# Four more matrices and whole down projections in split fp32r products, expert biases added by TensorE

## The reference, cut to what matters

```
# end of block 1 and of the mixer of block 2
x = x + concat([hm, ha]) @ w_out                  # 1024 x 1024
mix = (gate_a * y_a + gate_b * y_b) @ w_out_2     # 1024 x 1024
# block 3
proj = x @ w_in_3                                 # 1024 x 2048: pool value, b gate, c gate, conv value
mix = concat([y_pool, y_conv]) @ w_out_3          # 1024 x 1024
x = layer_norm(ALPHA * x + mix)
# mixture of experts: 32 experts, top 4, rows sorted into blocks of 128 of one expert each
gu = xb @ w_gu[e] + b_gu[e]                       # 128 x 1024 @ 1024 x 2048
gate = min(gu[:, :1024], 7);  up = clip(gu[:, 1024:], -7, 7)
yb = ((up + 1) * gate * sigmoid(1.702 * gate)) @ w_dn[e] + b_dn[e]
```

## Time and profile before

| | |
|---|---|
| median of 3 runs | 3586.9 us |
| profiled execution, its time and its span | 3590.4 us, 3588.6 us |
| TensorE busy in the span | 3244.0 us (90%) |
| VectorE, ScalarE, GpSimd busy | 53%, 41%, 16% |
| mean granted TensorE clock | 0.951 |
| the expert stage, about 2195 to 3420 us | VectorE near 85% busy, DMA near 400 GB/s |

### The profile page before, as it was taken

How to read it: one execution, slowest core, us unless ns; L and a number is a source line. 1 busy time by engine, 2 the same in 40 slices (tenths; PEclk the granted TensorE clock), 3 DMA queues, 4 the chain that set the end, 5 groups by cost and what they waited for, 6 DMA issues and landing times. The chain is left out here.

```text
span 3588.6 us, 37970 instructions
## 1 busy us (share of the span) xinstructions
PE 3244.0 (90%) x13384; PEld 2295.1 (64%) x13384; DVE 1889.2 (53%) x2272; ACT 1484.3 (41%) x1959; POOL 563.6 (16%) x305
## 2 busy tenths in 40 slices
PE   7977899998999796979998985999999999999976
PEld 6744488784455675658886445777777777777752
DVE  3266233513344405160033236888888888888825
ACT  4344244422445321132232013656656656656522
POOL 3400144440000342124442000000000000000010
PEclk9988999999999797999999987999999999999988
DMA  3333222231111121212235307999999999999840
GB/s 137 111 148 141 94 73 104 81 112 64 59 70 47 55 96 61 94 47 94 94 117 214 117 33 312 392 402 404 393 404 398 400 406 397 400 405 397 360 199 24
DMA packets 69954, 713.66 MB, mean 199 GB/s; under 512 B 7408, under 2 KB 7792, under 8 KB 29424
## 3 DMA queue, kind: packets, MB, share of 16 engines
q1 hardware_dynamic: 58704, 670.10, 47.1%
q0 software_dynamic: 7056, 25.69, 1.8%
q10 hardware_dynamic: 4112, 16.78, 1.2%
HBM read 672.17 MB, written 40.37 MB: 199 GB/s over the span
## 5 line engine op out<-in xcount | busy, mean ns | idle before, releaser
L136 POOL TENSOR_TENSOR ring_low<-ring,ff_ring_high 128x1024 fp32r<-128x1024 f32 x136 | 331.0, 2466 | 734.5 <-ACT ff_ring_high L131 734.5
L197 PE MATMUL psum<-ff_high,ff_ring_high 128*128 128x512 f32 x832 | 326.2, 392 | 23.1 <-DVE h_low L337 8.6
L199 PE MATMUL psum<-ff_high,ring_low 128*128 128x512 f32 x832 | 325.4, 391 | 0.0
L197 PE MATMUL psum<-ex_high,ex_rows_high 128*128 128x512 f32 x768 | 316.3, 412 | 6.8 <-DVE ring_low L2518 6.8
L199 PE MATMUL psum<-ex_high,ex_rows_low 128*128 128x512 f32 x768 | 301.9, 393 | 0.0
L198 PE MATMUL psum<-h_low,ff_ring_high 128*128 128x512 f32 x704 | 275.3, 391 | 0.0
L2518 DVE TENSOR_TENSOR ex_more_low<-ex_more,ex_high_in_x 128x2048 fp32r<-128x2048 f32 x96 | 219.4, 2286 | 70.4 <-ACT ex_high_in_x L2445 70.4
L2518 DVE TENSOR_TENSOR ring_low<-ring,ex_high 128x2048 fp32r<-128x2048 f32 x96 | 214.2, 2287 | 40.3 <-ACT ex_high L2445 40.3
L1497 PE MATMUL psum<-h,ring 128*128 128x512 f32 x512 | 224.0, 594 | 1.1 <-ACTq L1568 1.1
L2407 PE MATMUL psum<-ex_more,ex_act_t 128*128 128x512 f32 x512 | 224.9, 592 | 0.0
L2445 ACT ACTIVATE ex_high<-ex_more 128x1024 fp32r<-128x1024 f32 x192 | 200.8, 1063 | 57.3 <-PE psum L199 57.3
(11 more groups left out here) (512 smaller groups left out, 6440.0 us busy)
## 6 DMA issues: line engine op xcount, KB each, us to landing
ex_more<-moe_w SPq DMA_DIRECT2D x128, 2048.0 KB, 10.5
ring<-wstream SPq DMA_DIRECT2D x87, 2048.0 KB, 8.1
ring<-moe_w SPq DMA_DIRECT2D x64, 2048.0 KB, 11.8
ex_bias_up<-moe_b SPq DMA_DIRECT2D x32, 1024.0 KB, 8.3
y_rows<-ex_y SPq DMA_DIRECT2D x33, 512.0 KB, 9.0
y_rows<-mx_zero ACTq DMA_DIRECT2D x1, 16384.0 KB, 51.5
ex_bias_down<-moe_b SPq DMA_DIRECT2D x32, 512.0 KB, 8.3
x<-xt SPq DMA_DIRECT2D x8, 256.0 KB, 5.9
```

Of the source, the lines that this page charges most:

```text
L136: e.tensor_tensor(low, full, high.bitcast(F32), ALU.subtract).then_inc(self.low_ready, 1)
L197: pe.matmul(out, a[0], b[0], start=start, stop=False)
L199: return pe.matmul(out, a[1], b[0], start=False, stop=stop)
```

## The change

- `w_out`, `w_out_2`, `w_in_3` and `w_out_3` join `SPLIT` and are computed as split products. `Halves` makes the halves of an activation that no norm precedes, at the head of `out1` and `out2`. The mixer's norm gets halves (`keep` also keeps x itself), VectorE makes the low half of the first panel in between and GpSimd those of the later panels; the mixed tiles are split at the end of each panel's step, the low half on GpSimd.
- Expert stage: all 24 quarters are split, through a ring of twelve high quarters. The order is 0 to 15 as before, then (4,0), (4,1), (5,0), (5,1), (4,2), (4,3), (5,2), (5,3). The fp32 products are gone.
- VectorE now makes the low pairs n = 20 and 22 after `low_act(0)` and `take_up(1)`, and only then comes to `low_rows(0)`, `low_act(1)`, `low_rows(1)`.
- The biases are split once in `route_stage`, stored as two rows for each expert, and loaded as two rows; TensorE adds them with one fp32r matmul of ones for each bank (six a block). The steps that take the banks lose their bias operand, and `take_gate` and `take_up` one instruction each.

```diff
-SPLIT = ("w_in", "w_up", "w_down", "w_mix_a", "w_zv", "w_mix_b", "w_ffn_in", "w_ffn_out")
+SPLIT = ("w_out_3", "w_in_3", "w_out_2", "w_out", "w_in", "w_up", ... "w_ffn_out")
+class Halves:
+    def finish(self, act, t):
+        act.activation(tile_of(self.high, t), tile_of(self.full, t), ACT.Copy).then_inc(self.high_ready, 1)
+    def apply(self, dve, between):
+        for t in range(DT):
+            if between is not None:
+                between(t)
+            dve.wait_ge(self.high_ready, t + 1)
+            dve.tensor_tensor(tile_of(self.low, t), tile_of(self.full, t), tile_of(self.high, t).bitcast(F32), ALU.subtract)\
+                .then_inc(self.low_ready, 1)
 def dense_stage(...)  # ScalarE
+                if norm is not None and norm.interleave:
+                    for c in range(PARTS):
+                        if dve_lows:
+                            ring.high_part(act, n0, c)
+                        norm.finish(act, 2 * c)
+                        norm.finish(act, 2 * c + 1)
 def mixer_stage(...)  # GpSimd
+                norm.wait_tile(pool, DT - 1)
+                ring.low_done = n0 + 1
+                ring.low_until(pool, n0 + 3)
+                for j in range(4):
+                    low_tile(j, 2 * j + 1)
+                    low_tile(4 + j, 2 * j + 2)
+                    ring.low_until(pool, min(n0 + j + 4, n0 + 5))
 def route_stage(...)  # SyncE, behind the six pieces of the first expert
+                sp.wait_ge(bias_high_ready, 1)
+                sp.dma_start(r.bias_halves[:, 0, :], bias_high[:, :].bitcast(F32)).then_inc(bias_stored, 16)
+                sp.wait_ge(bias_low_ready, 1)
+                sp.dma_start(r.bias_halves[:, 1, :], bias_low[:, :].bitcast(F32)).then_inc(bias_stored, 16)
+                sp.wait_ge(bias_stored, 32)
 def expert_stage(...)
-    RING = 10
+    RING = 12
-    PIECES = ... + tuple((s, c) for s in (4, 5) for c in range(2))
+    PIECES = ... + tuple((s, 2 * a + c) for a in range(2) for s in (4, 5) for c in range(2))
-    act_at, dve_at = (14, 19), (8, 10, 14, 18)
+    act_at, dve_at = (14, 19, 20), (8, 10, 14, 18, 20)
 # TensorE
+                def add_bias(s, bank, added):
+                    at = (0, 2, 1, 3)[s] if s < 4 else s
+                    mm = pe.matmul(bank, ones[:, :], bias[:, at * PANEL:(at + 1) * PANEL], start=True, stop=False)
...
                     pe.wait_ge(h_done, b * 2 + 4)
                     turn_act(1)
                     pe.wait_ge(x_low, b * 2 + 3)
                     turn_rows(1)
                     for c in range(2):
                         quarter(b, 5, c, psum[:, 7, :], act_high, act_low)
-                    pe.wait_ge(a_ready, b + 1)
+                    pe.wait_ge(a_low, b * 2 + 2)
                     for s in (4, 5):
-                        for k in range(4, KT):
-                            mm = pe.matmul(psum[:, s + 2, :], act_t[:, k - 4, :], weights(s, k), start=False, stop=k == KT - 1)
-                        mm.then_inc(dn_done, 1)
+                        for c in (2, 3):
+                            quarter(b, s, c, psum[:, s + 2, :], act_high, act_low)
 # ScalarE
+                        if n == act_at[2]:
+                            sigmoid(b, 1)
...
-                    sigmoid(b, 1)
                     act.wait_ge(x_turned, b * 2 + 3)
                     high_rows(0)
-                    take_act(b)
+                    high_act(b, 1)
 # VectorE
                 def take_gate(b, c):
-                    dve.tensor_tensor(gate[:, :], psum[:, 2 * c, :], bias_up[:, 512 * c:512 * c + 512], ALU.add).then_inc(taken, 1)
-                    dve.tensor_scalar(gate[:, :], gate[:, :], SW_LIMIT, None, ALU.min).then_inc(limited, 1)
+                    dve.tensor_scalar(gate[:, :], psum[:, 2 * c, :], SW_LIMIT, None, ALU.min).then_inc(taken, 1)
...
+                        if n == dve_at[4]:
+                            low_act(b, 0)
+                            take_up(b, 1)
                         dve.wait_ge(high_ready, b * NQ + n + 2)
                         at = slice(c * PART, (c + 2) * PART)
                         dve.tensor_tensor(low_piece(s)[:, at], piece(s)[:, at], slots(n, 2).bitcast(F32), ALU.subtract)\
                             .then_inc(low_ready, 1)
-                    low_act(b)
-                    take_up(b, 1)
-                    for c in range(2):
-                        low_rows(b * 2 + 2 + c, c)
+                    low_rows(b * 2 + 2, 0)
+                    low_act(b, 1)
+                    low_rows(b * 2 + 3, 1)
```

More of the change, by code:

```diff
@@ L125, in split_parts, with high_part @@
             yield self.tile[:, n % SLOTS, part], self.high[:, n % SLOTS, part], self.low[:, n % SLOTS, part]
+    def high_part(self, act, n, c):
+        act.wait_ge(self.landed[n % SLOTS], 16 * (n // SLOTS + 1))
+        full, high, _ = list(self.split_parts(n))[c]
+        act.activation(high, full, ACT.Copy).then_inc(self.high_ready, 1)
     def high_panel(self, act, n, more=0):
@@ L378, in apply_raw, with __init__, wait_tile, averages @@
             dve.scalar_tensor_tensor(xt, xt, self.before(t), self.var, ALU.mult, ALU.mult).then_inc(self.raw_scaled, 1)
+class Halves:
+    def __init__(self, sem, name, full, high, low):
+        self.full, self.high, self.low, self.before, self.interleave = full, high, low, None, True
+        self.high_ready, self.low_ready = sem(f"{name}_high"), sem(f"{name}_low")
+    def wait_tile(self, e, t):
+        e.wait_ge(self.low_ready, t + 1)
+    def averages(self, pe):
+        pass
+    def finish(self, act, t):
+        act.activation(tile_of(self.high, t), tile_of(self.full, t), ACT.Copy).then_inc(self.high_ready, 1)
+    def deviations(self, dve):
+        pass
+    def apply(self, dve, between):
[5 more added lines that the diff above has]
+                .then_inc(self.low_ready, 1)
 class Tile:
@@ L1428, in block_1 @@
             Tile([n0 + t // 4], t % 4 * P, P, h, None, "dve",
-                 (lambda to: lambda e, bank: e.tensor_tensor(to, bank, to, ALU.add))(x[:, t, :])) for t in range(DT)],
-            n0 + 2 + SLOTS, split_to=FIRST["w_up"] + 1,
+                 (lambda to: lambda e, bank: e.tensor_tensor(to, bank, to, ALU.add))(x[:, t, :]), halves=(high, g.h_low))
+            for t in range(DT)],
+            n0 + 2 + SLOTS, split_to=FIRST["w_up"] + 1, dve_lows=True,
+            norm=lambda sem, scratch: Halves(sem, "mix", h, high, g.h_low),
             sums=lambda sem, buf, final: Sums(g, sem, x, buf, final, False))
@@ L1943, in _ @@
                 norm.averages(pe)
[L1944 removed]
                 for k in range(KT):
+                    ring.wait_part(pe, n0, k)
                     norm.wait_tile(pe, k)
                     for m in range(4):
[L1948 removed]
+                        mm = split_product(pe, psum[:, m, :], ring.halves(n0, k, m * P, P), tile_halves(x_high, x_low, k),
+                                           k == 0, k == KT - 1)
                         if k == KT - 1:
@@ L2072, in route_stage @@
         norm = norm(sem, in_row[:, :, :].rearrange("p (a c) r -> p a (c r)", a=4))
+        bias, bias_low = with_low(nc, own, "rt_bias", [NE, 3 * D])
+        bias_high = nc.alloc_sbuf_tensor_at("rt_bias_high", [NE, 3 * D], F32R, offset=g.h_at)
+        bias_in, bias_high_ready, bias_low_ready, bias_stored = (sem(n) for n in (
+            "bias_in", "bias_high_ready", "bias_low_ready", "bias_stored"))
         logit_taken = sem("logit_taken")
@@ L2750, in block_3 @@
     r.blanked = g.kept.enter_context(nc.semaphore("y_blanked"))
-    mixer_stage(g, x, h, r)
-    n0 = FIRST["w_out_3"]
-    dense_stage(g, "out3", [
-        Tile([n0 + t // 4], t % 4 * P, P, h, None, "dve",
-             (lambda to: lambda e, bank: e.tensor_tensor(to, bank, to, ALU.add))(x[:, t, :])) for t in range(DT)], n0 + 2, scale_x=x,
-                sums=lambda sem, buf, final: Sums(g, sem, x, buf, final, True))
+    r.bias_halves = nc.dram_tensor("bias_halves", [NE, 2, 3 * D], F32, kind="Internal").ap()
+    with ExitStack() as own:
+        high = g.open_split(own, "b3")
+        with nc.sbuf_tensor("b3_x_high", [P, DT, S], F32R) as x_high, nc.sbuf_tensor("b3_x_low", [P, DT, S], F32R) as x_low:
+            mixer_stage(g, x, h, r, high, x_high, x_low)
+        n0 = FIRST["w_out_3"]
+        dense_stage(g, "out3", [
+            Tile([n0 + t // 4], t % 4 * P, P, h, None, "dve",
+                 (lambda to: lambda e, bank: e.tensor_tensor(to, bank, to, ALU.add))(x[:, t, :]), halves=(high, g.h_low))
+            for t in range(DT)], n0 + 2, scale_x=x, split_to=n0 + 2,
+                    sums=lambda sem, buf, final: Sums(g, sem, x, buf, final, True))
     with ExitStack() as own:
```

169 lines of the change are left out of this document (100 added, 69 removed).

## The result

The changed kernel takes 3726.6 us (median of 4 runs, 3724.4 to 3729.5) against 3586.7 for the kernel before (4 runs beside it): a ratio of 1.0388, 95% interval 1.0376 to 1.0401. The profiled spans are 3588.6 and 3722.6 us, so +134.0.

| stretch | change | forecast |
|---|---|---|
| start to the last take of `out3` (2130.19 to 2085.57) | -44.6 | -45 |
| from there to the first transposes of the experts (2199.63 to 2166.94) | +11.9 | +11 |
| first to last transposes of the experts (1217.6 to 1386.9) | +169.3 | +151 |
| after them | -2.6 | 0 |

A forecast was written before the change was run, and what follows sets the result against it. TensorE was taken to do nearly all of the path. 3590.4 + 106 (stop) + 45 (clock) - 45 (matrices) + 11 (router's end) = 3707, less 3.5 for the median: 3704 us, range 3645 to 3750.

The forecast's parts named there:

- The stop: Expert stage: TensorE waits 3.77 us a block for `low_rows(0)`, T being the start of quarter n = 14; +106 us.
- The bank steps: Expert stage, VectorE: `take_gate` and `take_up` steps reading PSUM, taken as a copy's 0.69 us; 0.43 would make 8 us less.
- The clock: Expert stage: TensorE's clock falls after the stop, 1.7 us in four blocks of five, 1.4 on average; +45 us.
- The four matrices: `out1`, `out2`, `out3` and mixer: split products free TensorE time, less waits for halves; -45 us, bounds -57 and -35.
- The router's end: End of `route_stage`: bias-half stores issued behind 12.6 MB of weights delay the experts' first transposes; +11 us.
- TensorE's own work: Expert stage: four split quarters and six bias matmuls replace sixteen fp32 records, as long as before within 0.5 us.
- DMA: Expert stage: 1.5 MB of spread biases a block go, out of 15.2 MB; worth nothing, since nothing waited for DMA.

The follow-up runs named there:

- the best kernel: Changed kernel with bias stores before weights, low rows before pairs 20 and 22, `high_act` after quarter 20, `high_rows(0)` before quarter 22, `low_act(b, 1)` between those pairs: 3499.0 us.
- half dose: Changed kernel with one of the two second-half subtractions left ahead of `low_rows(0)` on VectorE and the other moved behind it: 3597.2 us.

## Why the prediction came out as it did

The time was 22.6 us above the 3704 forecast and inside the range. By its steps:

- **The stop: right.** Forecast: `turn_rows(1)` at T+11.96 behind pairs 20 and 22, 3.77 us late, and a period of 41.3 us at full clock. Measured: T+11.86, 3.67 us late, and 41.36 us where the clock was kept up by matmuls. That is +109 us for +106. The step from VectorE's start to TensorE's next instruction took 0.73 us, not 0.82. The bank steps took 0.68 us, as the copy out of PSUM did. The Trainium skill (VectorE: DVE Perf Modes, "Why PSUM operands drop a tier") says that an fp32 operand in PSUM gets no doubled rate, and the trace agrees: 0.68 us, where the step from SBUF takes 0.43.
- **The clock: the mechanism right, the size too small.** This is the term that was mis-sized: 1.4 us a block, 45 us, by one stretch at 1482 with its 1.7 us and a guess of four blocks in five. It is 1.84 us a block, 59 us. The discount to four blocks in five had no row behind it, and the changed kernel's trace shows no such discount: matmuls at 0.43 us stand behind the stop in each of the 32 blocks. At 1.7 us in every block the term would have been 54. The Trainium skill (TensorE: Matmul & The Clock Gate, "Loop structure matters more than you think") shows as its bad case a loop that waits 8 us for a DMA in every turn and then runs its matmul cold. The trace agrees for a stop of 3.5 us in every turn; stops of 1.42 and 1.30 us in every turn left the clock at 1.00.
- **The four matrices: right.** -44.6 for -45; `out1` and `out2` gave about 8.0 and 10.1 (8.3 and 10.0), mixer and `out3` together 25.6 (27). These make 43.7; the other 0.9 lie outside these stages. The run with them alone gives 39 by the medians, so that they agree to 0.4 us is partly luck of one pair of executions.
- **The router's end: right.** 10.6 us from the stores' place and 1.4 from slower steps of the router, for +11; moving the stores returned 11.0. The 12.4 us of the run with the stores first show that the stores' place is the cause.
- **TensorE's own work: right in sum.** "As long as before, within 0.5" stands: the best kernel, where TensorE never waits in a block, has a period of 36.43, and before it was 37.94 less the wait of 1.42, so 36.52; (4,0) starts at T+4.88, where it did before, so the two bias matmuls ahead of it went into its wait and cost nothing there.
- **DMA: right.** Nothing waited for it, and leaving the bytes out of the kernel before moved nothing.

By the spans, 14 us of the miss are the clock, 3 the stop, 1 the router, 1 the rest of the stage and 0.4 the matrices, less 2.6 behind the stage: 17. The other 5.7 us are the choice of executions: I took 3.5 off for a median below the profiled run before, and the changed kernel's profiled run was 2.2 us below its median.

What the prediction did not look for is an order that both kernels share. With all the orders put right the kernel is 50 us under the one that has only the dense matrices (3499.0 against 3549.1). That does not show that the expert stage's change is good in itself. The kernel with only the dense matrices still waits 45.3 us before (4,0), because ScalarE's `high_act` stands ahead of quarter 19, and the best kernel has that mended. TensorE's own work is the same in both but for 0.1 us a block (36.52 and 36.43), 3 us in all. So nearly all of the 50 us can be the old wait. Whether the kernel before gets it back by the same move, with its old expert stage, was not run. Nor was it separated what the biases and what the split second halves contribute: the one number is the 33.6 us that the bias matmuls cost in the best kernel.

## What to carry to other kernels

When work is added to an in-order engine's list, look up who waits for the step that it is put ahead of: here 4.4 us of subtractions went in front of a 0.6 us step that ended 0.3 us before it was needed, and 138 us hung on their order. Look for such waits in the kernel that you start from too: mending one that had been there already gave 41.5 us in the changed kernel. Price a stop of TensorE in a loop as its length plus the clock that falls behind it, and test the two apart with matmuls that nobody needs. Issue a small store ahead of large loads if a barrier waits for it: behind 12.6 MB of loads on the same queue it landed after 31.5 us instead of 7.7, and the next stage began 11 us later.

## What the runs showed of the hardware

- The same stop of 3.5 us is followed by a low clock of unequal length: TensorE's matmuls were at 0.43 us apiece from 2601.75 to 2606.99 in one block, and from 2645.87 to about 2648.0 in the next. Over the stage some 12, 4 and 8 matmuls take turns in this, and no block has none. In the blocks with 8 the transposes and the first matmuls behind the stop are still at full speed (four transposes in 0.66 us at 2558.03), and the lower level comes at 2559.27, 1.2 us after TensorE went on.
- Stops of 1.42 us (kernel before) and of 0.94 and 1.30 us (half dose), once in every block, left the granted clock at 1.00 over 1000 us.
- The DMA engines were shown 98% busy at 401 GB/s in a stage that they did not bound.
- While GpSimd made the low half of the biases in 6.70 us, one small step of VectorE, a `tensor_scalar` of 128x4, took 2.77 us and ended with it (2117.00 and 2116.97). In the kernel before, where GpSimd does nothing at that place, it took 0.17 us. The two steps in front of it, also beside GpSimd's, took 0.29 and 0.47 us as before. So it is not every step that is held.

```profile
2558.03 0.66 PE L2460 MATMUL psum<-const,ex_rows 128*128 128x128 f32 x4 [3.48 <-DVE ex_rows_low L2565]
...
2559.27 0.63 PE L202 MATMUL psum<-ex_high_in_x,ex_act_high 128*128 128x512 f32 x1
```

```profile
2110.27 6.70 POOL L2222 TENSOR_TENSOR rt_bias_low<-rt_bias,rt_bias_high 32x3072 fp32r<-32x3072 f32 x1 [21.19 <-ACT rt_bias_high L2237]
```

```profile
2113.40 0.29 DVE L2266 TENSOR_TENSOR rt_logits<-psum,rt_rb 128x128 f32<-128x128 f32 x1 [6.62 <-PE psum L2189]
2113.72 0.47 DVE L2271 MAX8 rt_best<-rt_logits 128x8 f32<-128x32 f32 x4
2114.23 2.77 DVE L2273 TENSOR_SCALAR rt_neg_top<-rt_best 128x4 f32<-128x4 f32 x1
```

The same step before:

```profile
2157.71 0.17 DVE L2184 TENSOR_SCALAR rt_neg_top<-rt_best 128x4 f32<-128x4 f32 x1
```
